# Queries leave PSUM ahead of the next split, additions to X come first at stages' ends, and Hyena's absolute sums a panel later

## What is computed

```python
def second_block(x, ...):                 # DEPTH_2 = 4, N_MIXERS = 3
    for i in range(DEPTH_2):
        kind, s = i % N_MIXERS, i // N_MIXERS
        h = rmsnorm(x, norm_mix[i])
        if kind == 0:
            y = hyena_mixer(h, ...)
        elif kind == 1:
            y = window_attention(h, ...)
        else:
            y = pool_mixer(h, ...)
        x = x + y
        x = x + swiglu_2(rmsnorm(x, norm_ffn[i]), ff_w_gate[i], ff_w_up[i], ff_w_down[i])
    return x
```

## Time and profile before

| what | value |
|---|---|
| three runs | 2973.93, 2975.38, 2977.11 us (median 2975.38) |
| the profiled execution | 2977.15 us, its span 2975.3 us, mean granted clock 0.988 |
| TensorE busy | 2902.9 us, 98% |
| weight loads of TensorE | 2684.5 us, 90% |
| VectorE busy | 2034.1 us, 68% |
| ScalarE busy | 1626.9 us, 55% |
| GpSimd busy | 277.3 us, 9% |
| read from HBM | 609 MB, 205 GB/s over the span |

### The profile page before, as it was taken

One profiled execution on the slowest core, in us unless ns is written; L12 is line 12 of the kernel. 1 busy time (PEld: TensorE's weight loads), 2 busy tenths in 40 slices (PEclk: granted clock), 3 DMA queues, 4 the chain that ended last, 5 costly groups with the idle time before them and its releaser, 6 DMA issues.

```text
span 2975.3 us, 46613 instructions
## 1 busy us (share of the span) xinstructions
PE 2902.9 (98%) x20144; PEld 2684.5 (90%) x20144; DVE 2034.1 (68%) x1842; ACT 1626.9 (55%) x1603; POOL 277.3 (9%) x224
## 2 busy tenths in 40 slices
PE   8999999999989999999999899999899999999999
PEld 8999999999978888888888687999799999886999
DVE  6787665678768888888888765554655465575553
ACT  6456544545657767767677552545654454462542
POOL 1130210123010000000000002100011011002110
PEclk9999999999999999999999999999899999999999
DMA  7444555544449989989899440556155646541453
GB/s 235 155 142 157 180 176 184 185 146 146 163 180 371 348 343 376 351 335 354 341 373 369 148 128 29 178 175 242 44 179 179 195 143 193 175 131 40 152 180 123
DMA packets 359730, 613.26 MB, mean 206 GB/s; under 512 B 11519, under 2 KB 323925, under 8 KB 324576
## 3 DMA queue, kind: packets, MB, share of 16 engines
q1 hardware_dynamic: 355936, 597.99, 57.7%
q10 hardware_dynamic: 3104, 12.10, 1.2%
q0 software_dynamic: 480, 0.12, 0.0%
HBM read 608.99 MB, written 1.05 MB: 205 GB/s over the span
## 4 chain that ended last, share of the span: by engine, by line
PE 91%; DVE 4%; ACT 3%; issue 1%; DMA 1%; ACTq 0%; SPq 0%; DVEq 0%
PE ps L329 18%; PE ps L330 18%; PE ps L331 18%; PE ps L1267 5%; PE ps L1269 5%; PE ps L1268 5%; PE ps L1245 3%; PE ps L1243 3%; PE ps L1244 3%; PE ps L1808 2%; PE ps L689 2%; PE ps L1823 2%; DVE wlo L273 2%; ACT whi L262 1%; PE ps L1317 1%; PE ps L1764 1%
## 5 line engine op out<-in xcount | busy, mean ns | idle before, releaser
L273 DVE TENSOR_TENSOR wlo<-raw,whi 128x2048 fp32r<-128x2048 f32 (+2 forms) x574 | 1317.8, 2300 | 584.1 <-ACT whi L262 579.7
L262 ACT ACTIVATE whi<-raw 128x2048 fp32r<-128x2048 f32 (+2 forms) x574 | 1084.4, 1891 | 261.2 <-PE ps L331 134.5
L329 PE MATMUL ps<-HX,whi 128*128 128x256 f32 x1808 | 524.3, 290 | 16.5 <-DVE wlo L273 11.7
L330 PE MATMUL ps<-HX,whi 128*128 128x256 f32 x1808 | 515.7, 285 | 0.0
L331 PE MATMUL ps<-HX,wlo 128*128 128x256 f32 x1808 | 515.4, 285 | 0.0
L329 PE MATMUL ps<-HXB,whi 128*128 128x256 f32 x1760 | 500.9, 285 | 6.7 <-DVE HXB L448 6.7
L330 PE MATMUL ps<-HXB,whi 128*128 128x256 f32 x1760 | 498.0, 283 | 0.0
L331 PE MATMUL ps<-HXB,wlo 128*128 128x256 f32 x1760 | 498.0, 283 | 0.0
L329 PEld LDWEIGHTS ps<-HX,whi 128*128 128x128 f32 x1808 | 351.1, 194 | 22.8 <-ACT HX L524 10.6
L330 PEld LDWEIGHTS ps<-HX,whi 128*128 128x128 f32 x1808 | 351.2, 194 | 3.2 <-issue 3.1
L331 PEld LDWEIGHTS ps<-HX,wlo 128*128 128x128 f32 x1808 | 351.2, 194 | 0.0
(11 more groups left out here) (337 smaller groups left out, 4232.9 us busy)
## 6 DMA issues: line engine op xcount, KB each, us to landing
raw<-in_c_experts SPq DMA_DIRECT2D x264, 1024.0 KB, 4.9
raw<-in_w_in SPq DMA_DIRECT2D x71, 1024.0 KB, 5.0
raw<-in_ff_w_gate SPq DMA_DIRECT2D x44, 1024.0 KB, 5.3
raw<-in_ff_w_up SPq DMA_DIRECT2D x44, 1024.0 KB, 5.3
raw<-in_ff_w_down SPq DMA_DIRECT2D x32, 1024.0 KB, 5.3
raw<-in_dense_w SPq DMA_DIRECT2D x30, 1024.0 KB, 5.3
raw<-in_hy_w_in SPq DMA_DIRECT2D x24, 1024.0 KB, 5.2
raw<-in_ff_w_down SPq DMA_DIRECT2D x16, 768.0 KB, 4.5
```

Of the source, the lines that this page charges most:

```text
L262: e.activation(m.whi[:, i % NSPLIT, 0:n], m.raw[:, i % NRAW, 0:n], ACT.Copy).then_inc(*k.up("act", "hi", i))
L273: e.tensor_tensor(m.wlo[:, i % NRAW, 0:n], m.raw[:, i % NRAW, 0:n], hi, ALU.subtract).then_inc(*k.up("dve", "lo", i))
L329: e.matmul(o, wh, xh, start=first and t == k0, stop=False)
L330: e.matmul(o, wh, xl, start=False, stop=False)
```

## The change

Five orders change; no arithmetic does. (1) `dve_out`, `dve_hyena` and `dve_ffn`: the last split of each turn goes behind the additions to X and the hx. (2) `FILTER_TURNS`: all turns but the first move one panel later, so that the L1 sums of filter 0 stand after panel 3 and those of filter 1 after panel 10. (3) Attention: in `queries` and `query_squares` the query leaves PSUM and is squared ahead of the next panel's split and whi. (4) Pooling: `pe_last_sums` goes ahead of the last group. (5) ScalarE's wait for "backward" goes ahead of the squares after the experts.

```diff
--- before.py
+++ after.py
@@ -923,7 +923,6 @@
 
 def dve_out(e, k, m, panels, s, nxt):
     for j in range(4):
-        dve_panel(e, k, m, panels)
         dve_add_x(e, k, m, s, "out", j)
         if s == "hgrn1":
             dst, x, gain = routed_rows(m, 2 * j + 1)
@@ -931,7 +930,9 @@
             e.tensor_scalar(dst, x, gain, None, ALU.mult).then_inc(*k.up("dve", "xg", s, 2 * j + 1))
         if j:
             dve_ahead(e, k, m, s, 2 * j - 2, 2, nxt)
-    dve_ahead(e, k, m, s, 6, 2, nxt)
+        if j == 3:
+            dve_ahead(e, k, m, s, 6, 2, nxt)
+        dve_panel(e, k, m, panels)
 
 
 def dve_conv(e, k, m, s, l, cs):
@@ -1078,7 +1079,7 @@
         if after:
             after(j)
     for j in range(4):
-        for part in range(3):
+        for part in range(2):
             dve_panel(e, k, m, panels)
         for c in (2 * j, 2 * j + 1):
             e.wait_ge(*k.at("y", s, c))
@@ -1087,7 +1088,9 @@
             k.note("dve", "x", s, c)
             if c:
                 dve_ahead(e, k, m, s, c - 1, 1, nxt)
-    dve_ahead(e, k, m, s, 7, 1, nxt)
+        if j == 3:
+            dve_ahead(e, k, m, s, 7, 1, nxt)
+        dve_panel(e, k, m, panels)
 
 
 
@@ -1706,7 +1709,7 @@
 PADS = 6
 PIECES = [(part, c) for part in range(2) for c in range(2)]
 
-FILTER_TURNS = {0: ("spec", 0, 3), 2: ("l1", 0), 3: ("spec", 1, 0), 4: ("spec", 1, 1), 5: ("spec", 1, 2), 6: ("spec", 1, 3), 9: ("l1", 1)}
+FILTER_TURNS = {0: ("spec", 0, 3), 3: ("l1", 0), 4: ("spec", 1, 0), 5: ("spec", 1, 1), 6: ("spec", 1, 2), 7: ("spec", 1, 3), 10: ("l1", 1)}
 
 
 def pads(m):
@@ -2274,8 +2278,8 @@
         e.activation(f, f, ACT.Exp, scale=-0.5).then_inc(*k.up("act", "hrs", s, n))
 
     def query_squares(j):
+        squares(1 + j, m.buf(0)[:, 512 * j:512 * j + 512], "q", j)
         act_panel(e, k, m, panels)
-        squares(1 + j, m.buf(0)[:, 512 * j:512 * j + 512], "q", j)
 
     def exps(g):
         e.wait_ge(*k.at("less", s, g))
@@ -2351,8 +2355,8 @@
             *k.up("dve", "normed", s, n))
 
     def queries(j):
+        dve_times_norm(e, k, m, s, last, "q", j, m.buf(0)[:, j * 512:j * 512 + 512])
         dve_panel(e, k, m, panels)
-        dve_times_norm(e, k, m, s, last, "q", j, m.buf(0)[:, j * 512:j * 512 + 512])
 
     def softmax(g):
         hs = slice(4 * g, 4 * g + 4)
@@ -2439,6 +2443,8 @@
     n = pe_panel(e, k, m)
     wh, wl = weights(m, n, 8, 256)
     for g in range(4):
+        if g == 3:
+            pe_last_sums(e, k, m, last)
         o = pe_take(e, k, m, "g", s, "in", g)
         for j in range(2):
             oj = o[:, j * 256:j * 256 + 256]
@@ -2451,7 +2457,6 @@
                 mm = e.matmul(oj, xl, wh[:, t, :], start=False, stop=t == 2 * g + 1)
         mm.then_inc(*k.up("mm", "g", s, "in", g))
     k.note("mm", "used", n)
-    pe_last_sums(e, k, m, last)
     pe_factors_down(e, k, m, s, last)
     Z, A = pool_views(m)
     e.wait_ge(*k.at("windows"))
@@ -2632,9 +2637,9 @@
     crowded(e, k, m, flag, act_crowded)
     k.note("o_act", "o end", "o_act")
     act_dft_load(e, k, m, a, "hy0")
+    e.wait_ge(*k.at("backward", "hy0"))
     for c in range(4):
         act_square(e, k, m, "moe", 2 * c, 2)
-    e.wait_ge(*k.at("backward", "hy0"))
     act_final(e, k, m, "final", "moe")
     act_hyena(e, k, m, a, panels, "hy0", "final", 0, before_ffn(m, "norm_ffn_2", 0))
     act_ffn(e, k, m, panels, "ffn1", "hy0", before_mixer(m, "norm_mix_2", 1))
```

## The result

The changed kernel takes 2983.61 us (median of 11 runs, 2981.8 to 2984.8) against 2976.42 us of the kernel before on the same chips: 1.0025 times the time, interval 1.0017 to 1.0032. It is slower by 7.2 us where 4.9 us faster was forecast (each figure is a difference to the kernel before). The profiled execution has a span of 2982.4 us, 7.1 more than the one before, so the trace holds the whole loss.

What follows compares the result with a forecast made beforehand. TensorE bounds the kernel, busy 2902.9 of 2975.3 us, its idle time at seams between stages. Terms -16.1 + 0.6 + 1.5 + 3 x 2.15 + 4 + 0.4 - 1.8 = -4.9 us gave 2970.5 us, range 2954 to 2977.

Steps and rivals of the forecast that it cites:

- The L1 sums: Both Hyena stages: sums a panel later end TensorE's waits there, gaining 8.26 + 7.79 = 16.1 us, the surest term.
- the 2.15 us of the forecast: Ends of ffn0 and ffn1: the split starts 0.02 us before L392, sums come late, +2.15 us each.
- forecast 339.7 and 2182.8: Times of the sums behind hgrn0 and attention, against 339.15 and 2181.30 before: +0.6 and +1.5 us.
- L392 of 3.4 us after hgrn0, attention: Sign of contention, also named for ffn0, ffn1 and ffn2: GpSimd's L392 waits out VectorE's split, with L380 waits of 2 to 3 us.
- rival 1: Three ffn ends: GpSimd is first, TensorE waits for nothing, -13.4 us in all, 2962 us; chance 0.23.
- The experts' +0.4: MoE behind hgrn1: the moved split makes L1411 start 0.8 us late, of which TensorE passes on +0.4 us.
- The Hyena ends: Ends of the Hyena outs: sums at 1872.4 against 1872.46 before, so a cost of 0.
- L392 is first: Hyena outs: GpSimd's L392 at 2.08 us after the last addition's start precedes the split at 2.37, so cost 0.
- Attention: Two queues reordered: query 3's norm and exponentials come earlier, -1.8 us, bounds -4 and +2.
- The clock: Four new TensorE waits of 2.2 to 2.9 us lower its clock, 1.0 us each, +4 us.
- pooling: Pooling stage: its sums start at 2373.9 instead of 2371.80, +2.15 us, despite being asked for one group earlier.
- Rival 3: Waits cool TensorE for long, 3.4 us each at five places and 3 more in attention: 2986 us, slower; chance 0.10.

Runs made afterwards that it cites:

- e1: The kernel before with the new FILTER_TURNS alone, the L1 sums one panel later: 2959.42 us, ratio 0.9943.
- e8: The changed kernel with one or two small one-input VectorE instructions between the two splits at the start of feed-forward stages: 2984.28 us, ratio 1.0023 to the kernel before.
- e7: The changed kernel with one or two small VectorE instructions ahead of the moved split at stage ends: 2970.13 us, ratio 0.9971 to the kernel before.
- e9: The kernel before with VectorE's half of the queries' move alone, a query leaving PSUM ahead of the split: 2972.89 us, ratio 0.9986.
- e11: The changed kernel with ScalarE's half of the queries' move undone, the high part before the squares again: 2975.94 us, ratio 0.9998 to the kernel before.
- e3: The kernel before with only attention's two reorderings, VectorE's and ScalarE's: 2980.40 us, ratio 1.0012.
- e4: The changed kernel, VectorE waiting for GpSimd's last addition of squares before the last split of each stage end but hgrn1's: 2956.32 us, ratio 0.9930 to the kernel before.
- e2: The kernel before with only the additions to X ahead of the split in dve_out, dve_hyena and dve_ffn: 2998.66 us, ratio 1.0072.
- e12: The changed kernel with one small two-input VectorE instruction between the two splits at four feed-forward stages' start: 2982.18 us, ratio 1.0021 to the kernel before.
- e5: The changed kernel with VectorE's wait for GpSimd's last addition of squares and both attention reorderings undone: 2951.59 us, ratio 0.9915 to the kernel before.

## Why the prediction was wrong

**What held.** The L1 sums: 7.46 us for sums and panel at clock 1.00, as counted (1.70 + 5.76), in both stages, and 17.3 us alone (e1) where 16.1 were forecast. The additions start earlier, as said. That the moved split (wlo from raw and whi, not "whi from raw") meets GpSimd's last additions held at every end and was the right thing to look for: the wait behind ffn0 and ffn1 is the 2.15 us of the forecast, and the sums behind hgrn0 and attention come where it put them (340.08 and 2183.08 when the lag ahead of them is taken off, forecast 339.7 and 2182.8). That these two times came out was luck in part. The count had L392 wait out one split (3.4 us) and L394 the other; L392 waited out both (5.50 us) and L394 ran at its own 0.72. The sum is nearly the same either way, as e8 shows, but "L392 of 3.4 us after hgrn0, attention" was a sign that didn't come. The lead of 0.02 us on which rival 1 rested was real (530.43 against 530.45), and e7 shows what the other order is worth. The experts' +0.4 came too (the lag is 7.57 at 850), and was given back by 880.

**The Hyena ends (+0 forecast, +6.4 measured).** The step that failed is "L392 is first". It does start first, by 0.28 us, but it starts while the fourth hx is still running. hx reads two operands in SBUF like the split, and holds GpSimd off like it; the 1.5 instead of 1.3 us of L392 there before was the sign, with hx running beside it:

```profile
1868.70 1.53 POOL L392 TENSOR_TENSOR work<-work 128x512 f32<-128x512 f32 x1 [4.69 <-ACT work L363]
```

VectorE's next instruction followed directly, and the next, and GpSimd was let in only behind the second split: 2.5 us at each of the two ends, the other 1.5 of the second's 3.9 being a stretch of low clock some 20 us earlier. I took the start of an instruction for the possession of what it needs. The Trainium skill (SBUF — State Buffer, "SBUF: two separate sides") gives the ports that the two engines share, for the whole instruction, to whichever starts first. The 5.89 us agree with the whole instruction; the start in the trace isn't the one that counts, since by it L392 was ahead of the split.

**Attention (-1.8 forecast, +4.6 measured).** The single times came out well: 11.18 us between queries 1 and 2 (forecast 2085.3 and 2096.4, so 11.1), exps(1) 1.1 us earlier against the lag (forecast 1.4). Two steps failed. First, I treated the move as one, and weighed its parts only against each other; apart, VectorE's half is worth 4.0 us (e9) and ScalarE's costs 7.7 (e11). The term to catch was in my own text: "whi, which ran ... in a gap, now follows". The 1.9 us of whi, out of their gap and on the path, put query 2 off by 2.35 us (11.18 against 8.83). Second, the gain was read off the exponentials and not off TensorE's own waits. TensorE's idle time in attention stayed at 11.7 us: the long wait of 4.3 us at query 3's head norm went, while one of 3.9 arose at query 2's and one of 3.0 at the scores (L2170), which wait for a PSUM bank that ScalarE frees behind exps(1). The 4.6 us are then all clock: busy time rose from 70.99 to 75.59 us, with the granted clock down from 0.90 to 0.86. Of these only part belongs to the order: e3 has the same order, the same waits and 1.3 us. So the two steps account for -1.8 forecast against +1.3; that the low clock took 3.3 us more in the changed kernel has no cause shown (by the same reading e4 has +2.9 and e8 +5.4, both with this order).

**The clock (+4 forecast).** Mis-sized, and of both signs. (The three waits it was taken from, 2.38, 2.67 and 1.89 us in the prediction, are 2.12, 2.41 and 1.73 us of idle time in the trace; the 1.0 doesn't hang on that.) After the 3 us wait behind hgrn0 a stretch that took 6.1 us before took 8.72 (0.67), so +2.7 where I took 1.0; behind ffn0, ffn1 and attention the lag grew by about 1.5 more than the wait; behind the first Hyena a wait as long (9.13 us for a panel of 5.76, less what the panel waited before) cost no clock at all. Nor does a place keep its price. In e2, e11 and e12 hgrn0's end costs 2.5 to 2.7 us where it costs 3.75 here, and in e8 0.9, with TensorE at 1.00 behind it; ffn0's costs 2.2 in all four where it costs 3.75 here; the first Hyena's costs 4.0 in e2 and e11 where it costs 2.5 here. TensorE's wait there is the same (2.9 us; 2.0 at ffn0's), in e8 and e12 0.15 to 0.25 shorter. In pooling the sign is the other one: its sums come late as forecast (the factors' turn at L477 comes 2.2 us later against the lag), but the stretch from the sums to the same later matmul has 0.83 on average and not 0.72 (with group 3 in it, which stood ahead of the sums before), and the net is -0.1. Attention's busy time differs by up to 6.3 us between the kernels above for the same matmuls. From such rows a term for the clock can be bounded (0 to 1.6 us a wait at the ends of ffn0, ffn1 and attention, up to 2.8 at hgrn0's), but not forecast per wait.

**The sum.** The two columns of the ledger are 12.2 us apart (12.1 between forecast and result): attention is 6.4, the Hyena ends 6.4, hgrn0's end 2.15, the other ends and the experts 1.2, less 2.3 at pooling and 1.7 in the Hyena stages. Rival 3 was nearest with its 2986 us, by a cause that holds only in part: it was to be TensorE's long cooling alone. Its 0.10, and the range's end at 2977, came from pricing the Hyena ends at the one value 0 and attention at +2 at worst, with no case in which both go wrong.

**What is open.** When GpSimd waits and VectorE has a second split ready, who is next? In the changed kernel GpSimd got in at the boundary of two splits at the three feed-forward ends (3.4 us), as in the earlier trace rows, and never at the four others (5.5 to 5.9 us), the same in each kernel of this order. The order of starts doesn't explain it (split ahead by 0.02 us at the feed-forward ends, by 0.05 to 0.06 within hgrn0 and once by 0.24: in; by 0.10 at the ends of hgrn0 and attention, and by 0.05 at hgrn0's in e7: out; behind by 0.02 at attention's in e7: out). A small instruction between the two splits let it in at eight of eight places (e8, e12); one ahead of the first split (e7) did so at the Hyena ends and not at hgrn0 and attn. What decides without one wasn't found.

## To carry to other kernels

When an instruction is moved out of a critical place, ask what it now runs beside: here a split with three panels in hand went next to the one GpSimd instruction that the next stage waits for, and a wait that costs nobody anything (e4) was worth 27 us. Price each swapped pair by itself: of the four parts that can be told apart here two gain and two lose (the additions first only without the guard), and the best kernel (2946.84 us, 0.9901) has the later L1 sums, the additions first with the guard, and VectorE's half of the queries' move, beside pooling's earlier sums and the moved wait, which were not run alone. Where two engines exclude each other, follow the waiting one through every boundary up to its last instruction, not only to its first.

## What the runs showed of the hardware

- GpSimd's `tensor_tensor` of 512 columns, 1.3 us alone, took up to 5.9 us beside VectorE's instructions with two SBUF inputs, and may miss the boundary between two that follow directly. VectorE is held up too: an instruction with two SBUF inputs on one column took 1.27 us (e12); the one with one input took 0.14 in the same place (e8).
- One small VectorE instruction, which delayed the split behind it by 0.07 us, changed a stage end by 3.7 us (e7 against the changed kernel): L392 took 1.30 us in place of 3.42.
- TensorE's granted clock can take more from a change than its waits do: with the idle time of attention at 11.7 and 11.6 us, the busy time was 75.59 (clock 0.86) and 70.99 us (0.90) for the same matmuls (changed kernel, e5). The same order and waits gave 72.44 us in e3.
- The same wait of TensorE (2.0 us at ffn0's end) was followed by a stretch of low clock in one trace and by none in four: the end cost 3.75 us in the changed kernel, with a granted clock of 0.83 over the next 10 us, and 2.2 us in e2, e8, e11 and e12, with 1.00.
